# A two-layer adaLN decoder trunk on one core: the order of work around its norms, and the buffers of its split weights

## What is computed

```python
for layer in range(2):
    mod = silu(c) @ ada_w[layer] + ada_b[layer]          # 6 vectors of 2048
    sh_m, sc_m, g_m, sh_f, sc_f, g_f = split(mod, 6)
    h = rmsnorm(x, norm_mix[layer]) * (1 + sc_m) + sh_m
    mix = attn_sgu_mixer(h, ...) if layer == 0 else short_conv_mixer(h, ...)
    x = x + g_m * mix
    h = rmsnorm(x, norm_ffn[layer]) * (1 + sc_f) + sh_f
    x = x + g_f * ((silu(h @ w_gate) * (h @ w_up)) @ w_down)   # inner width 5632
return rmsnorm(x, final_norm)
```

## Time and profile before

| | |
|---|---|
| median of 3 runs | 2347.69 us (2346.55 to 2348.88) |
| the profiled execution | 2347.18 us |
| its span | 2345.4 us |
| PE busy | 2255.0 us, 10172 matmuls |
| DVE busy | 1621.3 us |
| ACT busy | 1154.5 us |
| POOL busy | 104.4 us |
| read from memory | 612.02 MB |
| mean granted PE clock | 0.987 |

### The profile page before, as it was taken

How to read it: one execution, slowest core, us unless ns; L and a number is a source line. 1 busy time by engine, 2 the same in 40 slices (tenths; PEclk the granted TensorE clock), 3 DMA queues, 4 the chain that set the end, 5 groups by cost and what they waited for, 6 DMA issues and landing times.

```text
span 2345.4 us, 26716 instructions
## 1 busy us (share of the span) xinstructions
PE 2255.0 (96%) x10172; PEld 1863.4 (79%) x10172; DVE 1621.3 (69%) x1584; ACT 1154.5 (49%) x1501; POOL 104.4 (4%) x71
## 2 busy tenths in 40 slices
PE   3988999899999999999989999998999999999998
PEld 2777888688888888888878888886888888888886
DVE  5877888777887777677778777877744544544554
ACT  4666664578744334434455444446444433444443
POOL 0002301000000110000100000010000001000010
PEclk9998999999999999999999999999999999999999
DMA  9997779799788888888878878886866666666664
GB/s 324 352 315 283 290 253 314 274 334 323 277 321 284 289 306 299 286 289 301 285 242 285 297 278 284 291 296 211 290 184 189 190 191 193 195 187 192 188 189 134
DMA packets 286031, 615.90 MB, mean 263 GB/s; under 512 B 19792, under 2 KB 20176, under 8 KB 285520
## 3 DMA queue, kind: packets, MB, share of 16 engines
q1 hardware_dynamic: 284464, 613.50, 77.5%
q10 hardware_dynamic: 1440, 0.69, 0.1%
HBM read 612.02 MB, written 2.10 MB: 262 GB/s over the span
## 4 chain that ended last, share of the span: by engine, by line
PE 93%; DVE 3%; issue 2%; ACT 1%; DMA 1%; DVEq 0%; SPq 0%; ACTq 0%
PE ps L1247 30%; PE ps L1249 29%; PE ps L1248 29%; PE ps L1300 2%; DVE acc L877 2%; PE ps L1281 1%; DMA ada<-ada_w 1%; PE ps L1287 1%; DVE wlo L851 0%; ACT whi L517 0%; PE ps L1451 0%; PE ps L1406 0%; ACT hf L583 0%; DVE final L1212 0%; DVE tmp L972 0%
## 5 line engine op out<-in xcount | busy, mean ns | idle before, releaser
L851 DVE TENSOR_TENSOR wlo<-raw,whi 128x1024 fp32r<-128x1024 f32 x776 | 957.3, 1238 | 619.8 <-ACT whi L517 619.3
L517 ACT ACTIVATE whi<-raw 128x1024 fp32r<-128x1024 f32 x776 | 822.9, 1061 | 1059.4 <-PE ps L1249 1052.7
L1247 PE MATMUL ps<-whi,h 128*128 128x512 f32 x2144 | 856.1, 399 | 26.4 <-issue 21.5
L1249 PE MATMUL ps<-whi,h 128*128 128x512 f32 x2144 | 841.7, 393 | 0.0
L1248 PE MATMUL ps<-wlo,h 128*128 128x512 f32 x2144 | 841.6, 393 | 0.0
L1247 PEld LDWEIGHTS ps<-whi,h 128*128 128x128 f32 x2144 | 407.5, 190 | 116.8 <-issue 30.7
L877 DVE SCALAR_TENSOR_TENSOR acc<-ada,cact,acc 128x1024 f32<-128x1024 f32 x368 | 484.4, 1316 | 19.9 <-DMA ada<-ada_w 8.8
L1248 PEld LDWEIGHTS ps<-wlo,h 128*128 128x128 f32 x2144 | 407.8, 190 | 85.9 <-issue 3.6
L1249 PEld LDWEIGHTS ps<-whi,h 128*128 128x128 f32 x2144 | 406.6, 190 | 86.1
L1247 PE MATMUL ps<-whi,act 128*128 128x512 f32 x704 | 274.6, 390 | 0.0
L1249 PE MATMUL ps<-whi,act 128*128 128x512 f32 x704 | 273.9, 389 | 0.0
(11 more groups left out here) (118 smaller groups left out, 909.5 us busy)
## 6 DMA issues: line engine op xcount, KB each, us to landing
ada<-ada_w SPq DMA_DIRECT2D x384, 512.0 KB, 6.1
raw<-ff_gate SPq DMA_DIRECT2D x176, 512.0 KB, 4.1
raw<-ff_up SPq DMA_DIRECT2D x176, 512.0 KB, 3.9
raw<-ff_down SPq DMA_DIRECT2D x176, 512.0 KB, 4.0
raw<-conv_in SPq DMA_DIRECT2D x96, 512.0 KB, 5.0
raw<-w_in SPq DMA_DIRECT2D x88, 512.0 KB, 6.8
raw<-w_out SPq DMA_DIRECT2D x32, 512.0 KB, 6.5
raw<-conv_out SPq DMA_DIRECT2D x32, 512.0 KB, 5.8
```

What stands on the lines that cost most here:

```text
L517: nc.scalar.activation(whi[v % SPLIT][:, :, :], raw[:, v % RAW], ACT.Copy).then_inc(hi_ready, 1)
L851: nc.vector.tensor_tensor(wlo[v % SPLIT][:, :, :], raw[:, v % RAW], whi[v % SPLIT][:, :, :].bitcast(F32), ALU.subtract).then_inc(lo_ready, 1)
L1247: nc.tensor.matmul(to, high, whi[v % SPLIT][:, k, :], start=begin, stop=False, skip_group_check=on)
L1249: ins = nc.tensor.matmul(to, low, whi[v % SPLIT][:, k, :], start=False, stop=end, skip_group_check=on)
```

## The change

**Buffers.** `RAW` goes from 5 to 8, and six slots (`HIGH`) hold high parts where four did. The low part has no buffer of its own any more: `wlo` lies at the address of `raw`, and `lo_piece` writes the low part over the loaded piece. SP may load piece v once PE has used piece v-8, ACT may make high part v once PE has used v-6 (`consumed`). `mask` and `wst` move into the arena to make room.

**Quarters of norm 0.** PE does the quarter's two turns right after units 9, 15 and 21, ahead of the reduce of the sums; ACT makes the quarter at the end of the same unit's work (`norm_quarter`), the two high parts and gains first and then both copies for later turns; DVE makes its low parts after that unit's blocks of the modulation.

**Two units each side of a norm, by tokens.** `last_units`: the last two units ahead of each of norms 1 to 4 first do all of t = 0 (24 matmuls), then all of t = 1, with turn 0 between the two halves of the last unit. `tokens_unit`: the first two units behind norms 1 to 3 do t = 0 of both and then t = 1 of both, with the next turns between. `acc_done` becomes one semaphore for each t. Gain and shift of some turns go to DVE (`SCALED_VE`: turns 0 and 1 of norm 1, turns 0 and 2 of norms 2 and 3), four instructions for each. DVE and ACT handle the pieces of the two units inside `norm`; blocks of the modulation that belong there are done in between. Reduces keep off the four units around a norm (`BOUNDARY`): that of unit 60 goes to 62, those of 258, 259 and all others stay.

**The end.** Six of the eight output blocks are multiplied by the last gain before the last residual; then only the inverse root is applied, to t = 0 by DVE ahead of t = 1's residual, to t = 1 by two instructions of DVE and two of ACT.

Cut to its core:

```diff
-RAW = 5
-SPLIT = 4
+RAW = 8
+HIGH = 6
...
+BOUNDARY = [u + d for u in (U_F0, U_CI, U_F1) for d in (-2, -1, 0, 1)]
...
-    free = [v for v in range(u, U_END) if v - 4 not in SCORE_UNIT]
+    free = [v for v in range(u, U_END) if v - 4 not in SCORE_UNIT and v not in BOUNDARY]
...
-F_TURNS = {max(ADA_REDUCE[j][0] + 1, U_F0 + q - 1): q for j, (k, q) in QUARTER_OF.items() if k and q}
+F_TURNS = {max(ADA_REDUCE[j][0], U_F0 + q + 1): q for j, (k, q) in QUARTER_OF.items() if k and q}
...
+SCALED_VE = [(1, 0), (1, 1)] + [(k, i) for k in (2, 3) for i in (0, 2)]
...
-        whi = [sb(f"whi{s}", [P, 2, COLS], F32R) for s in range(SPLIT)]
-        wlo = [sb(f"wlo{s}", [P, 2, COLS], F32R) for s in range(SPLIT)]
+        wlo = nc.alloc_sbuf_tensor_at("wlo", [P, RAW, 2, COLS], F32R, offset=nc.sbuf_base - RAW * 2 * COLS * 4)
+        whi = [sb(f"whi{s}", [P, 2, COLS], F32R) for s in range(HIGH)]
...
+        def consumed(engine, v):
+
+            if v in CLOSING:
+                engine.wait_ge(acc_done[1], CLOSING[v] + 1)
+            else:
+                engine.wait_ge(piece_used, USED_TO[v + 1])
...
                 if v >= RAW:
-                    sp.wait_ge(lo_ready, v - RAW + 1)
+                    consumed(sp, v - RAW)
...
-                nc.vector.tensor_tensor(wlo[v % SPLIT][:, :, :], raw[:, v % RAW], whi[v % SPLIT][:, :, :].bitcast(F32),
+                nc.vector.tensor_tensor(wlo[:, v % RAW], raw[:, v % RAW], whi[v % HIGH][:, :, :].bitcast(F32),
...
             def norm(k, layer, sh, of, u):
 
-                lo_next(u - 1, 0)
-                residual(NORM_RES[k] + 6)
                 scale_gain(layer, sh + 1, 0, of)
                 scale_gain(layer, sh + 1, 1, of)
+                lo_next(u - 2, 0)
+                residual(NORM_RES[k] + 6)
                 mean(k, 0)
                 inverse(k, 0)
+                lo_next(u - 2, 1)
+                norm_scaled(k, 0, layer, sh)
+                norm_lo(k, 0)
                 residual(NORM_RES[k] + 7)
-                norm_lo(k, 0)
+                norm_lo(k, 1)
                 mean(k, 1)
                 inverse(k, 1)
-                norm_lo(k, 1)
+                lo_next(u - 1, 0)
+                lo_next(u - 1, 1)
+                norm_scaled(k, 2, layer, sh)
                 norm_lo(k, 2)
-                lo_next(u - 1, 1)
                 norm_lo(k, 3)
                 lo_next(u, 0)
                 norm_lo(k, 4)
+                ada_ops(u - 2)
                 lo_next(u, 1)
                 norm_lo(k, 5)
...
+            def tokens_unit(u, g, t, n, nu, of, k0=None, between=None):
+
+                if n == 0:
+                    begin(g, t)
+                for half in range(2):
+                    half_unit(u, g, t, n == 0, n == nu - 1, of, 4 * n if k0 is None else k0, half)
+                    if half == 0 and between is not None:
+                        norm_turn(*between)
+
+            def last_units(u, g, nu, of, k=None):
+
+                for t in range(2):
+                    for d in range(2):
+                        tokens_unit(u + d, g, t, nu - 2 + d, nu, of, None, (k, 0) if k and t and d else None)
...
-                norm_turn(k, 0)
                 norm_turn(k, 1)
-                begin(g, 0)
                 pe.wait_ge(h_ready, 8 * k + 1)
-                half_unit(u, g, 0, True, False, h, 0, 0)
-                norm_turn(k, 2)
-                half_unit(u, g, 0, True, False, h, 0, 1)
+                tokens_unit(u, g, 0, 0, 4, h)
+                pe.wait_ge(h_ready, 8 * k + 2)
+                tokens_unit(u + 1, g, 0, 1, 4, h, None, (k, 2))
                 norm_turn(k, 3)
-                begin(g, 1)
                 pe.wait_ge(h_ready, 8 * k + 3)
-                half_unit(u, g, 1, True, False, h, 0, 0)
-                half_unit(u, g, 1, True, False, h, 0, 1)
-                reduce_ada(u)
-                norm_turn(k, 4)
-                norm_turn(k, 5)
-                unit(u + 1, g, 1, 4, h, h_ready, lambda t: 8 * k + 4)
-                reduce_ada(u + 1)
+                tokens_unit(u, g, 1, 0, 4, h, None, (k, 4))
+                pe.wait_ge(h_ready, 8 * k + 4)
+                tokens_unit(u + 1, g, 1, 1, 4, h, None, (k, 5))
...
                 if n in REDUCE_AT:
+                    norm_turn(0, 2 * REDUCE_AT[n])
+                    norm_turn(0, 2 * REDUCE_AT[n] + 1)
                     reduce_cols(REDUCE_AT[n])
-                if n - 1 in REDUCE_AT:
-                    norm_turn(0, 2 * REDUCE_AT[n - 1])
-                    norm_turn(0, 2 * REDUCE_AT[n - 1] + 1)
...
+            for i in range(6):
+                t, n = i // 3, i % 3
+                nc.vector.tensor_tensor(final[:, 4 * t + n, :], x[:, t, COLS * n:COLS * n + COLS],
+                                        gfin[:, COLS * n:COLS * n + COLS], ALU.mult).then_inc(gained, 1)
```

More of the change, by code:

```diff
@@ L829, in _ @@
                 keep_row(u)
-            for n in range(3, 15):
+            for n in range(3, 14):
                 hi_next(U_CO + n, 0)
@@ L844, in _ @@
                 norm_std(4, t)
+            sa.wait_ge(rstd_ready, 10)
+            for n in range(2):
+                sa.wait_ge(gained, 3 + n + 1)
+                nc.scalar.activation(final[:, 4 + n, :], final[:, 4 + n, :], ACT.Identity, scale=rstd[:, 1:2]).then_inc(out_act, 1)
         @block.vector
@@ L1136, in _ @@
                 ada_ops(n)
-            for n in range(2, 15):
+                if n in REDUCE_AT:
+                    norm_lo(0, 2 * REDUCE_AT[n])
+                    norm_lo(0, 2 * REDUCE_AT[n] + 1)
+            for n in range(2, 14):
                 lo_next(U_OUT + n, 0)
@@ L1528, in _ @@
                 reduce_ada(u)
-            for n in range(2, 16):
+            for n in range(2, 14):
                 if n < 4:
```

208 lines of the change are left out of this document (111 added, 97 removed).

## The result

The changed kernel takes 2309.61 us (median of 4 runs, 2309.18 to 2310.88), the kernel before 2347.35 beside it (4 runs, 2346.55 to 2348.88). The ratio is 0.9839, with a 95% interval of 0.9822 to 0.9856: 37.7 us faster, where 2311 was forecast. The profiled execution took 2309.18 us, of which the span is 2307.4.

A forecast was written before the change was run, and what follows sets the result against it. PE was taken as the bound, busy 2255.0 of 2345.4 us, so at most 90 us idle plus half-clock losses could be won. Terms 15 + 9.5 + 4.7 + 2.8 + 3.5 + 0.6 = 36.1 us gave 2311 us, range 2300 to 2327.

The forecast's parts named there:

- The quarters: Norm 0: the 4.31 us waits ahead of units 11, 17 and 23 go, DVE then holds the reduces; 15 us gained.
- Buffers: Steady stretches: deeper `raw` and `whi` costed at nothing, since PE has no gap there; low part in place the same subtraction.
- second rival: "The handovers don't move": at the norms PE waits mid-list or the wait is only cut in two; 2327 us, chance 0.14.
- slower: Rival: the low part's subtraction in place runs slower than the one now; about 2375 us at two thirds more, chance 0.04.
- Norm 1: Handover around norm 1: PE's loss falls from 12.8 us to 3.3; 9.5 us gained.
- Norm 2: Handover around norm 2: PE's loss falls from 9.0 us to 4.3; 4.7 us gained.
- norm 3: Handover at norm 3: gap ahead of the row reduce grows from 2.06 us to about 4; 2.8 us gained, between 0 and 6.
- The end: Behind the last matmul: shorter chain after the last residual, stores' issues taking back 0.4 us; 3.5 us gained.
- The start: Start of the program: the second half of quarter 0 is one copy earlier; 0.6 us gained.
- signs of being wrong: `wlo` mean away from 1238 ns, ACT `whi` waiting for loads in the quarters, PE idle inside a unit before a norm.
- The channel holds the quarters: Rival: the memory channel stays at 325 GB/s in norm 0's quarters and their term falls to nothing; 2326 us, chance 0.12.
- DVE takes all of it back: Rival: in the quarters of norm 0 DVE takes back all of the gain; 2321 us, chance 0.04.

The follow-up runs named there:

- the four others: Four kernels with quarters and attention exactly as in the changed one, edited elsewhere; they gain 17.4, 17.3, 17.7 and 17.3 us from unit 0 to unit 30.
- The late reduce: Changed kernel with units 258 and 259 also closed to reduces, so norm 3's row reduces come behind units 260 and 261: 2308.15 us (one run).
- DVE's order: Changed kernel with two DVE moves behind norms: second piece's low part before t = 0's residual, skipped blocks before turn 0: 2307.88 us (one run).
- DVE lighter: Changed kernel where DVE adds only half the columns of 30 modulation blocks in quarters 2 and 3, all loads kept: 2302.49 us (one run).
- the faster pace's kernel: Changed kernel with 36 instead of 32 modulation blocks done by unit 8: 2301.05 us, ratio 0.9804 to the kernel before.
- all three edits: Changed kernel with 36 blocks by unit 8, norm 3's later row reduces and the two DVE moves behind norms together: 2295.16 us, ratio 0.9779.

## Why the prediction was right

The measured 2309.61 us lie 1.4 below the forecast. **What bounds the kernel** held: all of the gain is gaps and time at half clock, and the stretches in which PE had no gap gave nothing.

**The quarters**, 15 forecast, 18.5 measured. The chain of steps came within 0.7 us everywhere: DVE's blocks start at 112.7 (113.0 forecast), the reduce at 140.4 (140.8), the next at 182.2 (181.5), unit 23 at 191.20 (191.2). But two gaps of about 5 us were forecast ahead of the reduces, and they are 4.10 and 1.74. In between PE is held up by the half clock, which the chain left out there: over the 8 us from 144 it was granted 0.63. DVE sets the time of that reduce either way, and it came 0.7 us late. The sum stopped one step too soon. Before, the third wait of 4.31 us lowered the clock for unit 23 itself; without it unit 24 is another 2.6 us ahead (lead 14.64 at unit 23, 17.25 at unit 24). The clock had been counted where a wait stayed and not where one went. Another 0.9 came from attention, where a wait for `qkT` fell from 1.68 to 0.81 us; it goes with the six slots, and was not in the sum at all. And about 1 us of the 18.5 is this execution's own, by the four others.

**Buffers**, nothing forecast for the steady stretches, and nothing there it is. But "costed at nothing" hid that the handovers stand on them: take the two extra slots away and norms 1 to 3 lose 3.6 us where they gained 17.1. The sum for the norms has no term for it. The wait of 3.24 us that came back is the prediction's second rival, "PE waits in the middle of its own list"; it was right in kind, and six slots are what keeps it away. The in-place subtraction costs nothing (1233 and 1238 ns), so the rival *slower* fell.

**Norm 1**, 9.5 forecast and measured, but the exact hit is luck: two waits of 1.1 and about 1 for `h` came as 1.25 each, and the third of 1.1, for a low part of the third unit, didn't come. **Norm 2**, 4.7 and 4.0; **norm 3**, 2.8 and 3.6. The waits were foreseen as 0.7, 1.7, 0.6 and 1.3 us and came as 0.82, 1.18, 0.83 and 0.94. The last was to be in the third unit, for the sixth low part of `h`; it came two units later, for the low part of a piece. They were summed as losses, 4.3 us; the waits were shorter than that, 3.8, and the loss still 5.0, for the reason given with the rows above. Gain and shift on DVE take 0.34 us each, nearer the upper bound of 0.17 to 0.37 than the 0.27 taken:

```profile
1553.67 1.37 DVE L962 TENSOR_SCALAR hf<-ps,gsc,mod 128x128 f32<-128x128 f32 x4 [0.51 <-PE ps L1365]
...
1579.55 2.67 DVE L899 SCALAR_TENSOR_TENSOR acc<-ada,cact,acc 128x1024 f32<-128x1024 f32 x2
```

The pair of blocks that the row reduce waits for ends at 1582.2, and PE's gap there grew to 3.85 us, "about 4". The late reduce and DVE's order show that DVE's list, not the reduce's place alone, set it.

**The end**, 3.5 forecast, 2.7 measured. The step that was short is the stores: DVE and ACT are done at 2303.6, 4.3 us behind the last matmul where 8.2 had passed before, so the arithmetic gained 3.9; but from there to the end of the span are 3.8 us where there were 2.7, so the stores hold back 1.2 where 0.4 was set. Half of that is the issues, which end at 2304.6. **The start** was forecast at +0.6 and came at -0.35; over the other runs it lies between -0.4 and 0.4, so the copy gives nothing that can be told from the spread of a start.

So the total is right partly by luck: 3.5 us too few in the quarters and 0.8 in norm 3 stand against 0.7 too many in norm 2, 0.8 at the end and 1 at the start.

**The signs.** Of the signs of being right, the gaps ahead of units 11, 17 and 23 are gone and the reduces wait for `acc`, the second far less than forecast; the end has 8.1 us, not under 8. Of the signs of being wrong one did show: ACT waited for loads in the quarters, four times for 1.8 to 2.4 us. It had been set too strictly, since these waits end before DVE needs the piece; what tells the two theories apart is a gap on DVE.

**The rivals.** *The channel holds the quarters* fell for this change: DVE has no gap ahead of the late reduce, and with DVE lighter the loads came at 388 GB/s. The stretch also asked less of the channel than reckoned: it moved 351 GB/s over 91.3 us, which is 32.0 MB, not the 34.5 counted from the kernel before. The Trainium skill's figure of about 358 GB/s ("DMA: Bandwidth & Descriptors", Specifications), weighed in the prediction, is passed here for 45 us on end. The same page's section Bandwidth ties it to both cores of a pair streaming, and this program runs on one; that the other core's traffic makes the difference was not tried. *The handovers don't move* and *DVE takes all of it back* fell by the table of leads; the first comes true with four high parts.

## What to carry to other kernels

When work is reordered so that two operands' users come later (all of one half of the rows, then all of the other), count the slots that stay held across the turn before pricing the order; with two slots too few this order was a loss. A wait ahead of PE can cost its length and then again, by the lower clock behind it: removing one of 4.1 us gave 8.6. Shorter waits may or may not; the rows below have both. And when a wait for an engine's queue stands at a fixed place while the queue idles earlier, move part of its work ahead in the table, until the loads say stop: one changed number gave 8.6 us more.

## What the runs showed of the hardware

- The rate of loads from memory reached 388 GB/s over 45 us in one kernel and 387 in another, each time at a share of 1.05 of the DMA engines' time.
- After a wait of 4.10 us the reduce of 16 matmuls took 3.57 us where the one without a wait took 1.84, and over the 8 us from 144 PE was granted 0.63, a mean of its two levels, 1.2 and 2.4 GHz, with PE busy throughout.
- The same length of wait can cost clock or not. Behind a wait of 1.97 us the faster pace's kernel was granted 0.79 over the 8 us from 172; with all three edits, behind one of 1.95, the same window has 1.00. The changed kernel's waits of 0.8 to 1.25 us at the norms cost none: from 187.5 to 1583 us it was granted 1.00.
- A `TENSOR_SCALAR` of 128x512 in float32 from SBUF takes 0.42 us (1.27 for three), a `TENSOR_TENSOR` of that size 0.69 (`x<-x,tmp`). The Trainium skill ("VectorE: DVE Perf Modes", The perf-mode tier table) gives the first twice the rate of the second for 2048 elements; the two rows, of 512, agree with the direction, at a factor of 1.6. That makes it worth multiplying by the last gain early: what is left behind the last residual is mostly the cheap kind, where a block with both factors takes 0.69 (2.74 for four).
